# Norm scales in column halves, and the first three high halves of a residual norm written by VectorE

## What is computed

```python
h = h + 0.5 * rms_norm_2(swiglu(rms_norm_2(h, g[0]), ffn_w13[i, 0], ffn_w2[i, 0]), g[1])
hn = rms_norm_2(h, g[2])
m = gmlp_mixer(...) if i == 0 else rwkv7_mixer(...)
h = h + rms_norm_2(m, g[3])
h = h + 0.5 * rms_norm_2(swiglu(rms_norm_2(h, g[4]), ffn_w13[i, 1], ffn_w2[i, 1]), g[5])
gate = jax.nn.sigmoid(rms_norm_2(h, g[6]) @ ple_w_gate[i])
h = h + rms_norm_2(gate * (p[i] @ ple_w_proj[i]), g[7])
```

## Time and profile before

| | |
|---|---|
| median of 3 runs | 3309.39 us (3308.82 to 3311.72) |
| the profiled execution, its own time | 3309.65 us |
| its span, first to last instruction | 3307.9 us |
| mean granted TensorE clock | 0.996 |
| PE busy | 3238.4 us, 98% |
| DVE busy | 1780.5 us, 54% |
| ACT busy | 1215.3 us, 37% |
| POOL busy | 97.2 us, 3% |

### The profile page before, as it was taken

How to read it: one execution, slowest core, us unless ns; L and a number is a source line. 1 busy time by engine, 2 the same in 40 slices (tenths; PEclk the granted TensorE clock), 3 DMA queues, 4 the chain that set the end, 5 groups by cost and what they waited for, 6 DMA issues and landing times.

```text
span 3307.9 us, 46956 instructions
## 1 busy us (share of the span) xinstructions
PE 3238.4 (98%) x20540; PEld 2650.9 (80%) x20540; DVE 1780.5 (54%) x2117; ACT 1215.3 (37%) x1535; POOL 97.2 (3%) x100
## 2 busy tenths in 40 slices
PE   9999999999999999999999999999999999999998
PEld 7878786888878888988788887888777787788886
DVE  6447665776354435364644357443476665754437
ACT  3347543222232223432322235222235554332224
POOL 2000000000000001000100011000000000100001
PEclk9999999999999999999999999999999999999999
DMA  5211131222322223222222222222212100122231
GB/s 203 71 52 64 64 140 51 96 96 91 101 91 101 94 88 112 102 79 100 96 90 94 96 90 90 102 90 92 97 61 85 38 4 16 70 104 100 87 105 64
DMA packets 46701, 286.49 MB, mean 87 GB/s; under 512 B 6161, under 2 KB 6433, under 8 KB 20769
## 3 DMA queue, kind: packets, MB, share of 16 engines
q1 hardware_dynamic: 44960, 280.34, 24.2%
q0 software_dynamic: 1536, 3.15, 0.4%
HBM read 278.22 MB, written 2.10 MB: 85 GB/s over the span
## 4 chain that ended last, share of the span: by engine, by line
PE 80%; DVE 5%; ACT 1%; issue 1%; DVEq 0%; ACTq 0%
PE ps L510 71%; PE ps L3308 3%; PE ps L3346 1%; PE ps L1220 1%; DVE wl L331 1%; PE ps L984 1%; DVE xl L2782 1%; PE ps L1221 1%; PE ps L1222 0%; ACT wh L315 0%; PE ps L2612 0%; DVE xl L1078 0%; PE ps L838 0%; DVE tmp L2790 0%; PE ps L3353 0%
## 5 line engine op out<-in xcount | busy, mean ns | idle before, releaser
L510 PE MATMUL ps<-xh,wh 128*128 128x512 f32 (+1 forms) x2464 | 965.3, 392 | 14.4 <-DVE xl L2782 6.2
L510 PE MATMUL ps<-xl,wh 128*128 128x512 f32 (+1 forms) x2464 | 945.7, 390 | 0.3
L510 PE MATMUL ps<-xh,wl 128*128 128x512 f32 (+1 forms) x2464 | 919.6, 390 | 0.0
L331 DVE TENSOR_TENSOR wl<-raw,wh 128x2048 fp32r<-128x2048 f32 (+2 forms) x283 | 589.1, 2082 | 445.3 <-ACT wh L315 445.1
L315 ACT CAST wh<-raw 128x2048 fp32r<-128x2048 f32 (+1 forms) x280 | 485.8, 1735 | 292.0 <-PE ps L510 288.2
L510 PEld LDWEIGHTS ps<-xh,wh 128*128 128x128 f32 (+1 forms) x2464 | 462.1, 188 | 125.3 <-issue 20.9
L510 PEld LDWEIGHTS ps<-xl,wh 128*128 128x128 f32 (+1 forms) x2464 | 461.6, 188 | 100.7 <-DVE xl L1078 2.8
L510 PEld LDWEIGHTS ps<-xh,wl 128*128 128x128 f32 (+1 forms) x2464 | 461.7, 188 | 98.7 <-issue 1.0
L510 PE MATMUL ps<-hid_h,wh 128*128 128x512 f32 x880 | 342.8, 390 | 0.0
L510 PE MATMUL ps<-hid_h,wl 128*128 128x512 f32 x880 | 342.4, 389 | 0.0
L510 PE MATMUL ps<-hid_l,wh 128*128 128x512 f32 x880 | 342.4, 389 | 0.0
(11 more groups left out here) (443 smaller groups left out, 4010.4 us busy)
## 6 DMA issues: line engine op xcount, KB each, us to landing
raw<-in_up SPq DMA_DIRECT2D x88, 1024.0 KB, 4.7
raw<-in_down SPq DMA_DIRECT2D x64, 704.0 KB, 4.0
raw<-in_up_c SPq DMA_DIRECT2D x22, 1024.0 KB, 4.7
raw<-in_down_c SPq DMA_DIRECT2D x16, 704.0 KB, 4.0
raw<-in_gates SPq DMA_DIRECT2D x8, 1024.0 KB, 4.7
raw<-in_gv SPq DMA_DIRECT2D x8, 1024.0 KB, 4.8
raw<-in_gu SPq DMA_DIRECT2D x8, 1024.0 KB, 4.7
raw<-in_gout SPq DMA_DIRECT2D x8, 1024.0 KB, 4.7
```

The costliest lines, as they stand in the source:

```text
L331: nc.vector.tensor_tensor(wl[:, slot, 0:w], raw[:, slot, 0:w], wh[:, slot, 0:w].bitcast(F32), ALU.subtract).then_inc(lo_ready, 1)
L510: last = nc.tensor.matmul(out, stationary, moving, start=(fresh and q == 0), stop=(t == kt - 1 and half == per - 1 and q == 2), skip_group ...
```

## The change

Root, reciprocal and spread are made in two halves of 64 columns each; each half of the spread has two lots, and each lot waits for the lot before it. The values wait for all eight spread products. ACT's root stands ahead of the waits for last products, PSUM read and addition, and waits for the sums alone. The fillers become one ahead of the last PSUM read, one behind it, and two (three without `onto`) behind the spread.

In the six Deferred norms with `onto`, ACT makes three tiles of h times the coming gain (`GainedAhead`) in the last unit of the stage before (down, gout, ple_gate0, rout), into the last three tiles of `xl` or into an area of their own. DVE then writes the high halves 0 to 2 itself, as value times gain plus that tile. POOL adds all eight tiles to `h`. The low half of tile t-1, in place of t-2, stands in step t on DVE. In `Beside` one unit of the embedding product stands ahead of the spread in place of two. The core of the diff:

```diff
@@ class Pass, square_root
             if self.quarters:
                 self.wait(act, n_sum, KD if self.by == "tensor" else 1)
-                nc.scalar.activation(self.total[:, 0:P], self.sums, ACT.Sqrt, scale=REPEAT * REPEAT / D,
-                                     bias=spare[:, 3:4]).then_inc(n_root.sem, 1)
+                for cols in COLUMN_HALVES:
+                    nc.scalar.activation(self.total[:, cols], self.sums[:, cols], ACT.Sqrt, scale=REPEAT * REPEAT / D,
+                                         bias=spare[:, 3:4]).then_inc(n_root.sem, 1)
                 return
@@ class Pass, spread
-                self.wait(pe, n_scale, 1)
-                for n, b in enumerate((0, 2, 1, 3)):
-                    if n == 2:
-                        self.wait(pe, n_spread, 2)
...
+                for half, cols in enumerate(COLUMN_HALVES):
+                    self.wait(pe, n_scale, half + 1)
+                    for n, b in enumerate((0, 2, 1, 3)):
+                        if n == 2 or half and n == 0:
+                            self.wait(pe, n_spread, TB * half + n)
...
@@ class Pass, invert
-                self.wait(dve, n_root, 1)
-                nc.vector.reciprocal(self.total[:, P:2 * P], self.total[:, 0:P]).then_inc(n_scale.sem, 1)
+                for n, cols in enumerate(COLUMN_HALVES):
+                    self.wait(dve, n_root, n + 1)
+                    nc.vector.reciprocal(self.total[:, P + cols.start:P + cols.stop], self.total[:, cols]).then_inc(n_scale.sem, 1)
@@ class Deferred, split_act
+            if self.post:
+                self.post.square_root(act)
             act.wait_ge(chunks_used, self.multiplied)
             act.wait_ge(psum_read.sem, self.evicted)
             act.wait_ge(dve_steps.sem, self.two.summed)
-            if self.post:
-                self.post.square_root(act)
...
-            for t in range(KD):
+            for t in range(self.gained_ahead.count if self.gained_ahead else 0, KD):
@@ class Deferred, pe
                 self.post.sum_up(pe)
+                keep_busy(pe, 1)
                 pe.wait_ge(psum_read.sem, self.evicted)
-                keep_busy(pe, 3)
+                keep_busy(pe, 1)
                 self.post.spread(pe)
-                keep_busy(pe, 5 if self.post.onto else 3)
+                keep_busy(pe, 2 if self.post.onto else 3)
@@ class Deferred
+        def tiles_onto(self, dve):
+            direct = self.gained_ahead.count
+            for t in range(KD):
+                self.post.gained(dve, t)
+                if t == 1:
+                    self.low(dve, 0)
+                if t < direct:
+                    self.high_from_sum(dve, t)
+                if t >= 2:
+                    self.low(dve, t - 1)
+            self.low(dve, KD - 1)
+
+        def high_from_sum(self, dve, t):
+            self.post.wait(dve, n_value, t + 1)
+            self.gained_ahead.wait(dve, t)
+            nc.vector.scalar_tensor_tensor(self.split(t)[0], self.post.scratch(2 + t % 2), vec[:, self.gain + t:self.gain + t + 1],
+                                           self.gained_ahead.tile(t), ALU.mult, ALU.add).then_inc(n_high.sem, 1)
+
         def pool(self, pool):
             if self.post and self.post.onto:
-                for t in range(1, KD):
+                for t in range(KD):
                     self.post.add_on_pool(pool, t)
@@ class GainedAhead
+        count = 3
...
+        def act(self, act):
+            for t in range(self.count):
+                nc.scalar.activation(self.tile(t), h[:, t, :], ACT.Copy,
+                                     scale=vec[:, self.gain + t:self.gain + t + 1]).then_inc(n_ahead.sem, 1)
@@ class Beside, pe
             self.lots.products(pe, 1, 0, 2)
-            self.lots.products(pe, 2, 0, 2)
             self.post.spread(pe)
-            for unit in range(3, KD):
+            for unit in range(2, KD):
                 self.lots.products(pe, unit, 0, 2)
```

More of the change, by code:

```diff
@@ L784, in act @@
             act.wait_ge(dve_steps.sem, self.summed)
-            for t in range(0 if self.by == "before" else KD):
-                self.square(act, t, before)
-            self.square_root(act)
+            if self.by != "before":
+                for t in range(KD):
+                    self.square(act, t, before)
+                self.square_root(act)
             if self.split:
@@ L2324, in gain, with in_low, in_area, ahead @@
         return VEC["norm"] + (layer * 8 + n) * KD
-    def feed_forward(layer, n, norm, between={}):
+    low_area = place("low_area", [P, GainedAhead.count, T], offset=x_at + (2 * KD - GainedAhead.count) * T * 4)
+    def in_low(t):
+        return low_area[:, t, :]
+    gained_area = area("gained_area", [P, GainedAhead.count, T], 40 * KB)
+    def in_area(t):
+        return gained_area[:, t, :]
+    def ahead(layer, n, where):
+        return GainedAhead(gain(layer, n), where)
+    def feed_forward(layer, n, norm, between={}, then=None):
         linear(f"up_{layer}{n}", KD, 256, x_split, norms=norm, between=between, paired="filled", **swiglu(norm))
         linear(f"down_{layer}{n}", HALF, P, hid_split, halves=True, norms=Made(lambda t: 4 * t + 4),
-               **summing(ybuf, 1))
+               between={KD - 1: (then.act, None)} if then else {}, **summing(ybuf, 1))
     def post(source, layer, n, total=None):
         return dict(source=source, gain=gain(layer, n), onto=True, total=total)
-    def pre(layer, n, after, lead=0):
-        return Deferred(gain(layer, n), post=after, lead=lead)
+    def pre(layer, n, after, lead=0, gained_ahead=None):
+        return Deferred(gain(layer, n), post=after, lead=lead, gained_ahead=gained_ahead)
     pt = area("pt", [P, 2, T], 88 * KB)
@@ L2490, in dve, with embed @@
             self.lots.low(dve, 0)
-            for t in range(KD):
-                self.post.gained(dve, t)
-                if t == 0:
-                    self.post.add_first(dve)
-                if t == 1:
-                    self.low(dve, 0)
-                if t >= 3:
-                    self.low(dve, t - 2)
-            self.low(dve, KD - 2)
-            self.low(dve, KD - 1)
-    def embed(layer, norm):
+            self.tiles_onto(dve)
+    def embed(layer, norm, then=None):
         def project(act, unit, product):
@@ L2672, in gmlp @@
                behind={0: turn_gain, **{unit: mix(unit) for unit in MIXES}})
-        linear("gout", KG, P, lambda t: (y_h[:, t, :], y_l[:, t, :]), norms=Landed(g_low), **summing(ybuf, 1))
+        linear("gout", KG, P, lambda t: (y_h[:, t, :], y_l[:, t, :]), norms=Landed(g_low),
+               between={KD - 1: (then.act, None)}, **summing(ybuf, 1))
     hn, dx = area("hn", [P, KD, T], 0), area("dx", [P, KD, T], 16 * KB)
@@ L3774, in dve @@
                 lower(KD - 1)
-        linear("rout", KD, 256, x_split, norms=HeadNorms(), paired="filled", **summing(sg, 2))
+        linear("rout", KD, 256, x_split, norms=HeadNorms(), paired="filled", between={3: (ahead_11.act, None)}, **summing(sg, 2))
     rwkv()
-    feed_forward(1, 1, pre(1, 4, post(r_out, 1, 3)), embedding(1))
-    embed(1, Beside(gain(1, 6), post(ybuf, 1, 5)))
+    feed_forward(1, 1, pre(1, 4, post(r_out, 1, 3), gained_ahead=ahead_11), embedding(1), then=ahead_last)
+    embed(1, Beside(gain(1, 6), post(ybuf, 1, 5), ahead_last))
     last_values, last_adds, last_pool = roles("last_values", "last_adds", "last_pool_adds")
@@ L3800, in _ @@
         last.invert(dve)
-        last.wait(dve, n_spread, 4)
+        last.wait(dve, n_spread, 2 * TB)
         for t in range(KD):
```

85 lines of the change are left out of this document (47 added, 38 removed).

## The result

The changed kernel takes 3357.18 us (median of 4 runs, 3356.32 to 3358.64) against 3309.11 (3308.38 to 3311.72): ratio 1.0139, 95% interval 1.0126 to 1.0151, 48 us slower. The forecast was 3340.0 in 3324 to 3356: slower was right, by 30 us where it is 48, and the time lies 1.2 us above the range (as a ratio on the 3309.39 shown before the forecast it is 3355.4, just inside). The profiled execution took 3358.64 around a span of 3356.9.

The account below looks back on a forecast made before the run. The prediction took PE, busy 98% of the span, to bound the kernel. It added 2.9 us for halves at five passes and 27.6 at six places, 30.5 in all, to 3309.65, giving 3340, range 3324 to 3356.

Parts of the forecast that it names:

- The slack of 0.3: Second norm at up_01: DVE's squares end 0.3 us before PE's first sum product; taken alike elsewhere, except 1.2 at gv.
- the same squares behind them: At the gates PE has 7 us of other products, then waits for the second norm's squares; 4.6 us lost each.
- Not slower: Rival, 0.13: the first high half decides at six places, each winning 0.7 or 1.5 us; 3305 to 3310.
- Value 0 to 0.75, xh 0 to 1.53, POOL's addition 0 behind it: First turns after the first gained value starts: DVE's high half ends at 1.53 us, then POOL's addition at 2.7.
- POOL first: Rival, 0.08: POOL gets the turn in the first three pairs, xl 7 ends at 23.3; +2.3 at six places, 3354.
- the sum had 27.6: Six Deferred norms with the addition: shift of the first value plus 4.8 us less slack, together 27.6 us slower.
- The clock falls: Rival, 0.17: PE's new waits lower the granted clock, 3.4 us lost per dip, two to five dips; 3347 to 3357.
- The forecast of 2.3 us idle ahead of the sums: PE waits some 2.3 us for DVE's squares ahead of the second norm's sums (L801).
- Part 1: Root, inverse and spread in halves, eleven norm passes: four spread lots take 2.0 us; the five plain passes lose 2.9 us.
- Fewer fillers cost and win nothing: In the norms, fewer filler products change no time by themselves, since PE waits for DVE there.
- The root behind its sums: Where a copy follows the sums (gv, up_01, up_11, first pass ahead of rr), the earlier root wins 0.28 us.
- Part 3: Three tiles scaled ahead on ACT, about 2 us, hidden by idle time; +0.25 in ple_gate0, at most 0.5 in rout.

Follow-up runs that it names:

- b_lag1: Kernel before with only the low half of tile t-1 instead of t-2 in step t, in Deferred (gates keep theirs): 3316.16 us, ratio 1.0018.
- a_first_on_dve: Changed kernel with tile 0's addition to h on DVE, behind its high half, instead of on POOL: 3348.38 us, ratio 1.0113.
- a_dve_wins: Changed kernel with POOL's additions 0 and 2 held until DVE's high half of that tile is done: 3340.08 us, ratio 1.0086.
- highs_alone: Changed kernel with root, inverse and spread whole again (root still early) and the low half of tile t-2 in step t: 3328.00 us, ratio 1.0050.
- b_new_fillers: Kernel before with only the fillers of the change: 3312.89 us, ratio 1.0004.
- whole: Changed kernel with root, inverse and spread whole again, the low half of t-1 kept: 3341.38 us, ratio 1.0091.
- lag2: Changed kernel with the low half of tile t-2 instead of t-1 in step t: 3333.52 us, ratio 1.0070.

## Why the prediction was right in sign and short by 17 us

**The mechanism holds, at four of the six places.** There PE is bound at the second norm's sums by a queue DVE, POOL, ACT that takes longer; the first high half gains nothing. The slack of 0.3 is right: in b_lag1 low 7 is 1.72 later and up_10 and up_11 lose 1.55. At the gates, where I had "the same squares behind them", PE waits for high halves of late tiles and then for a split of weights behind them, not for the squares, which end at 2002.53, 0.3 ahead of the first sum product; the queue DVE, POOL, ACT is the same, and the loss of 5.3 each is near the 4.6 of the sum. "Not slower", whose premise is that the first high half decides, is refuted by a_first_on_dve and a_dve_wins: high 0 at T0 + 1.53, as the change wants it, and still 28 to 38 us slower than before.

**The step that failed is "Value 0 to 0.75, xh 0 to 1.53, POOL's addition 0 behind it".** POOL got the first turn, and the third, and that is the rival "POOL first", to which I gave 0.08. I had the row against myself: DVE's own wait 0.02, POOL's 0.08. It led me to think that 0.04 to 0.06 ahead is ahead. DVE lost two of the first three pairs at every place, low 7 ended at 21.5 and not at 20.0, and that is worth 9 us at six places (gv, the gates and up_11 differ by 1.5 to 1.6 each between dve_wins and the kernel after). The rival's time, 3354, was 3 us low, and that is luck: it had low 7 at 23.3 and all three pairs the other way, where it is 21.5 and two of three.

**A term hidden by another error.** With the order as I had it, low 7 ends at 20.0, where I worked out 20.96: low 1 is recorded 0.15 ahead of POOL's addition 2 and gets the turn, so it is done at 7.4 and not 8.3, and POOL's addition 3 follows addition 2 at once. (The price of a turn for POOL was off too: the addition that waited at up_01 ends at 1599.68, 1.13 behind DVE's low half at 1598.55, not 1.25.) The six places measure 24.5 us in dve_wins, where the sum had 27.6; low 7 alone would take off 5.8, but at up_11 the clock fell behind a wait of 1.43 us there as well. That kernel's 3340.08 is the forecast time to 0.1 us; part of that is one term too large and another too small.

**The clock.** "The clock falls" was a rival of its own, of 0.17, and it came on top. The forecast of 2.3 us idle ahead of the sums is right at up_01, up_10 and up_11 (2.17, 2.26, 2.17), and 1.37 at gv; the gates have none. Behind all three longer waits the clock fell to 0.72 for 6 us. Against dve_wins, up_01 loses 1.85 and up_10 1.5 more than the 1.5 of low 7: 3.4 us. The other fall, at the start of the stream, costs nothing by itself: highs_alone has it too, clock 0.76, and up_01 still loses just the 2.6 that low 7 explains. That is so only while the queue leaves PE waiting anyway: in b_new_fillers the same fall costs 0.8 at gv and at up_11.

**Part 1 was mis-sized at the plain passes.** Forecast 2.9 us for the five, measured 7.1 in the kernel after. At full clock, from the sums' end to the first value, they take 0.78 (ln_ffn, and up_00 with the fillers of before), 0.98, 0.97 (ahead of rr) and 0.89 (last) more: 4.4. From the first product of the spread to the value it is 2.16 us against 1.15, since half the columns save little of a lot (0.44 against 0.49) and there are two lots more; and three fillers let the spread start only 0.04 to 0.24 sooner. The rest is the clock, 2.3 of it at up_00. At the six other places the terms were right: 0.3 at gv, up_01 and up_11 (forecast 0.2; up_01 has 0.26 more by the clock), 0.48 at up_10 (0.45) and 0.1 at the gates (0.1). "Fewer fillers cost and win nothing" is right for the time of the kernel before and wrong beside four lots: at up_00 the clock falls to 0.83 and 2.3 us go. The root behind its sums wins its 0.28 only when the fillers are also gone from ahead of the spread (2.71 against 2.93).

**Part 3** (tiles scaled ahead) can't be told from nothing: up_10's term of 0.25 is smaller than what one execution's clock does there.

**The sum.** 30.5 forecast. Add 12.5 at the six places for order of turns and clock, take off 3.1 for the terms that were too large, add 4.2 for the plain passes: 44. The profiled execution lost 49.0. The 4.9 left lie at the start, ahead of any changed instruction (2.2), in rr (2.4) and in small pieces. There other kernels' profiles stand from -0.8 to +2.6 and from -1.8 to +2.2 whatever was changed in them, so I can't assign them. That the four runs of the kernel after all lie above 3356 speaks against pure chance; what moves the clock in rr stays open.

Together the parts don't add: 7.7 (halves) + 17 (high halves) + 5 (order, at four of six places) + 1 (fillers) is 31, and the whole is 48. The order of t-1 costs 14 us in a whole norm (1.0091 less 1.0050) and 23 with halves (1.0139 less 1.0070), against 5 in b_lag1. At the six places the table has it alike in both companies, 16.2 (whole less highs_alone) and 18.4 (after less lag2): low 7 moves by 2.4 us at six places there, by 1.7 at four in b_lag1, and the clock falls behind the longer waits. What else makes 23 of 14, and 16 of 7.7 for the halves, lies mostly at the start, ahead of rr and in rr; no run shows why.

## What to carry to other kernels

Where VectorE and GpSimd take turns, an order that rests on 0.04 us, as here, is not an order: write it with a wait, or give both operations to one engine. A queue written out by hand should have its last item's time worked out, not its first one's. Cutting an instruction into halves pays only if its time is in its columns: the inverse's was (0.95 to 0.57), that of a lot of the spread was not (0.49 to 0.44).

## What the hardware showed that was not expected

Who gets the turn: with DVE's recorded start 0.04 us ahead POOL ran first, in high 0 and high 2 at all six places; with 0.15 ahead (1597.81 and 1597.96) DVE did. It is close enough to go either way: of the 30 first pairs of this kind in five kernels POOL won 29, and DVE one (gv in a_lag2, at 0.05, a lead with which it lost elsewhere), where high 0 ended at T0 + 1.54 and low 7 0.5 sooner. The Trainium skill says that issue order decides who blocks (SBUF — State Buffer, "Who interferes with whom"). The trace agrees that one of them blocks for the whole instruction, but the order of the recorded starts is not the order of turns when they are 0.04 apart. The pairs with 0.04 are all high halves and those with 0.15 all low halves, so whether the lead or the kind of operation decides is not shown.

The clock behind a wait of PE ahead of the second norm's sums, over the kernels with such waits: it fell in 11 of 12 waits of 2.12 to 2.26 us, and in 2 of 10 waits of 1.15 to 1.59. The same wait in the same place (1.15 at up_01, up_10 and up_11 of b_lag1) cost 1.7 us once and nothing twice.
